# Opening of a streaming encoder on one core: place of the first value-weight transfer, and identity products on TensorE ahead of the first two tiles

## The reference, cut to what matters

```
hp = rms_norm(xp, norm_mix[0]);  hs = rms_norm(xs, norm_mix[0])
qkv = (xn @ w_qkv).reshape(b, t, 3, N_HEADS, HEAD_DIM)
s = einsum('bqhd,bkhd->bhqk', q, k) * scale + bias
p = softmax(s);  o = einsum('bhqk,bkhd->bqhd', p, v);  x = x + o @ w_o
```

## Time and profile before

| | |
|---|---|
| median of 3 runs | 1281.15 us (1277.71, 1281.42, 1281.15) |
| profiled execution, its own time | 1276.23 us |
| its span, first to last instruction | 1274.6 us |
| TensorE busy | 1072.0 us, 84% |
| VectorE, ScalarE, GpSimd busy | 493.7, 289.5, 272.3 us |
| chain that ended last | TensorE 58%, DMA 21%, VectorE 10%, issue 8% |
| mean granted TensorE clock | 0.931 of 2.4 GHz |

### The profile page before, as it was taken

The page is one execution under the profiler, slowest core; times in us unless marked ns, Lnnn a source line. Parts: engine busy times, 40 slices in busy tenths (PEclk is TensorE's granted clock), DMA queues, the critical chain, the costliest instruction groups (busy, mean ns, idle before and its releaser), DMA issues.

```text
span 1274.6 us, 14578 instructions
## 1 busy us (share of the span) xinstructions
PE 1072.0 (84%) x5326; PEld 621.2 (49%) x5326; DVE 493.7 (39%) x1066; ACT 289.5 (23%) x616; POOL 272.3 (21%) x289
## 2 busy tenths in 40 slices
PE   6999999998996978777746999987986978787780
PEld 5777777774545333333315777653544333333320
DVE  3234444344356211111115799984554111111116
ACT  3233232333111101000003455553111101000002
POOL 3000000001003211001051488850003111100033
PEclk9999999999997989888887999998996989998895
DMA  8953322302707999999955912000037999999963
GB/s 279 389 174 110 109 96 78 105 25 106 297 34 280 412 420 419 421 421 421 391 165 141 374 37 71 25 25 12 32 108 290 396 421 421 421 420 421 378 258 131
DMA packets 110287, 303.68 MB, mean 238 GB/s; under 512 B 18440, under 2 KB 65672, under 8 KB 86521
## 3 DMA queue, kind: packets, MB, share of 16 engines
q1 hardware_dynamic: 87977, 254.74, 51.8%
q0 software_dynamic: 22256, 48.22, 10.4%
HBM read 278.34 MB, written 57.12 MB: 263 GB/s over the span
## 4 chain that ended last, share of the span: by engine, by line
PE 58%; DMA 21%; DVE 10%; issue 8%; ACT 2%; SPq 1%; POOL 0%; DVEq 0%; POOLq 0%
PE bank L1205 12%; PE bank L522 10%; DMA ring<-in_w_up 8%; DMA arena<-in_w_up 8%; PE bank L421 7%; PE bank L1224 6%; PE bank L549 4%; DVE bank L1711 2%; PE bank L1507 2%; PE bank L572 2%; PE bank L1195 2%; PE bank L588 2%; PE bank L613 2%; PE bank L346 1%; DMA work<-in_w_pw 1%
## 5 line engine op out<-in xcount | busy, mean ns | idle before, releaser
L1205 PE MATMUL bank<-ring,work 128*64 128x512 f32 x704 | 170.1, 639 | 30.4 <-DMA ring<-in_w_up 28.6
L1224 PE MATMUL bank<-ring,work 128*64 128x512 f32 x528 | 125.5, 619 | 36.2 <-DVE work L1243 23.8
L1507 PE MATMUL bank<-arena,work 128*128 128x288 f32 x512 | 129.6, 416 | 8.0 <-issue 3.6
L522 PE MATMUL bank<-arena,ring 128*128 128x288 f32 x512 | 131.9, 412 | 0.4 <-issue 0.4
L1205 PEld LDWEIGHTS bank<-ring,work 128*64 128x64 f32 x704 | 58.4, 147 | 139.3 <-issue 136.9
L1239 DVE TENSOR_TENSOR work<-work,bank 128x256 f32<-128x256 f32 x33 | 13.9, 420 | 287.9 <-ACT work L1235 287.9
L1507 PEld LDWEIGHTS bank<-arena,work 128*128 128x128 f32 x512 | 99.2, 195 | 37.9 <-issue 8.0
L1658 POOL TENSOR_TENSOR ring<-ring 128x606 f32<-128x606 f32 x76 | 103.6, 1363 | 55.3 <-ACT ring L1607 45.7
L522 PEld LDWEIGHTS bank<-arena,ring 128*128 128x128 f32 x512 | 94.9, 190 | 33.0 <-issue 8.4
L421 PE MATMUL bank<-ring,arena 128*128 128x512 f32 x224 | 101.2, 605 | 6.6 <-ACT arena L1642 6.6
L1205 PE MATMUL bank<-arena,work 128*64 128x512 f32 x352 | 86.2, 646 | 19.7 <-DMA arena<-in_w_up 18.7
(11 more groups left out here) (258 smaller groups left out, 1297.7 us busy)
## 6 DMA issues: line engine op xcount, KB each, us to landing
ring<-in_w_down SPq DMA_DIRECT2D x32, 2048.0 KB, 24.5
ring<-in_w_gate SPq DMA_DIRECT2D x20, 2048.0 KB, 21.6
ring<-in_w_up SPq DMA_DIRECT2D x20, 2048.0 KB, 30.7
arena<-in_w_gate SPq DMA_DIRECT2D x10, 2048.0 KB, 22.5
arena<-in_w_up SPq DMA_DIRECT2D x8, 2048.0 KB, 32.8
ring<-in_w_qkv SPq DMA_DIRECT2D x24, 512.0 KB, 6.1
y_sorted<-gain POOLq DMA_DIRECT2D x8, 1536.0 KB, 5.7
work<-in_w_pw SPq DMA_DIRECT2D x16, 512.0 KB, 5.2
```

The costliest lines, as they stand in the source:

```text
L522: mm = nc.tensor.matmul(bank[b][:, 0:HT], wa[s][:, w, c, :], xt[:, c, h * HT:(h + 1) * HT], start=c == 0, stop=c == C - 1)
L1205: mm = nc.tensor.matmul(bank[2 + s][rr, :], xte[s][:, c, rr], wgu[g][:, :, e, c, :], start=c == 0, stop=c == C - 1)
L1224: mm = nc.tensor.matmul(bank[5 + h][rr, :], hts[:, c, rr], wdn[s][:, e, c, h * HALF:(h + 1) * HALF], start=c == 0, stop=c == FC - 1)
L1507: mm = nc.tensor.matmul(bank[banks[h][w]][:, 0:GT], wp[s][:, w, c, :], xt[:, c, h * GT:(h + 1) * GT], start=c == 0, stop=c == C - 1)
```

## The change: where the value weights are asked for, and 33 identity products

Three edits. The request for the value weights of pair 0 is made behind that for tile 1, so ahead of tiles 2, 3 and 4; the same 512 KB go to the same place. TensorE multiplies the identity by itself 30 times before the transposes of tile 0, and 3 times between the transposes of tile 0 and of tile 1, into bank 5, which is first used when the head pairs begin. `keep_running` takes the bank as an argument, and keeps its old one elsewhere.

```
             # attn_pe
+            keep_running(30, 5)
             for j in range(TILES):
+                if j == 1:
+                    keep_running(3, 5)
                 turn_pe(pe, 0, j)
...
             # attn_sync
-            sp.dma_start(wa[0][:, 2, :, :], wq[:, :, 2 * D:2 * D + P]).then_inc(wv_in, 16)
...
-        def keep_running(count):
+        def keep_running(count, b=3):
             for _ in range(count):
-                nc.tensor.matmul(bank[3][:, 0:P], ident[:], ident[:], start=True, stop=True)
+                nc.tensor.matmul(bank[b][:, 0:P], ident[:], ident[:], start=True, stop=True)
...
             # block.sync
                 if j == 0:
                     sp.dma_start(gain[:, 0, :], broadcast(norm_mix[0])).then_inc(gain_in, 16)
+                if j == 1:
+                    sp.dma_start(wa[0][:, 2, :, :], w_qkv[0, :, 2 * D:2 * D + P].rearrange("(p c) n -> p c n", c=C)).then_inc(wv_in, 16)
```

## The result

The changed kernel takes 1285.38 us (median of 11 runs, 1283.35 to 1289.09) against 1281.42 us for the kernel before, measured beside it (11 runs, 1277.71 to 1284.12). The ratio is 1.0029, 95% interval 1.0017 to 1.004: 3.7 us slower, with 2.2 to 5.1 us in the interval (the two medians are 4.0 us apart; the ratio is an estimate over all runs). Forecast were 2.25 us. Its profiled execution took 1285.83 us, with a span of 1284.2 us.

What follows compares the result with a forecast made beforehand. It took q0's wait for pair 0's cached keys, landing at 29.09 us behind bias_rows, to cancel the opening's gain; 0 for all three edits plus 2.25 us for the clock on 1280.6 gave 1282.9 us, range 1277.5 to 1286.5.

Steps and rivals of the forecast that it cites:

- what bounds the opening: Before q0: the 0.43 us hole marked issue is the wait for pair 0's cached keys, landing at 29.09 us.
- The second rival: At q0: it doesn't wait for the keys, 3.4 us gained, time 1277.2 us; chance 0.08.
- Fillers, tile 0, tile 2, end of the opening: TensorE's opening: fillers end 11.5, tile 0 turned 11.5, tile 2 normed 16.05, last value product ends 25.6 us.
- The clock's cost: q0 to k1, 64 records: clock falls behind 3.5 us of idle, costing 2.25 us (bounds 0 and 3.0).
- The value weights cost nothing: Request order on the DMA queue: bias_rows and cached keys land unchanged, 0 us at 29.09, plus or minus 0.5.
- a sign of being wrong: At q0: prediction is wrong if q0 starts before 28 us or the keys' landing moves by more than 1 us.
- The last rival: Opening's transfers: keys land later as DMA engines run dry; from 1.6 us on, 1284.5 us and more; chance 0.08.
- The sum: Whole kernel: 0 for weights, fillers and earlier value products, plus 2.25 us for the clock; 1282.9 us, 0.18% slower.
- the third rival: Fillers before tile 0: they stay at 1.2 GHz and take 14.1 us; time 1282.1 to 1296 us; chance 0.04.
- a cap of 3.5 us: Pair 1's projection: its keys land at 42.8 us, projection starts at 46.38, limiting the second rival's gain.

Runs made afterwards that it cites:

- the bridge: Changed kernel with 18 more identity products between the last value product and q0: ratio 1.0014 to the kernel before.
- weights alone: Kernel before with only the value weights' request moved behind tile 1, no identity products: ratio 1.0034 to the kernel before.
- fillers alone: Kernel before with only the 33 identity products, value weights requested in their old place: ratio 1.003 to the kernel before.
- changed, keys early: Changed kernel with the request for pair 0's cached keys ahead of bias_rows: ratio 1.0003 to the kernel before.
- changed, keys and pair 1 early: Changed kernel with pair 0's cached keys ahead of bias_rows and pair 1's loads ahead of the wait for bias_rows: ratio 0.9968 to the kernel before.
- before, keys and pair 1 early: Kernel before with pair 0's cached keys ahead of bias_rows and pair 1's loads ahead of the wait for bias_rows: ratio 0.9997.
- fillers alone, small bridge: Kernel before with the 33 identity products and 6 more between the last value product and q0: ratio 1.0006 to the kernel before.

## Why the prediction was right, point by point

**The hole is the wait for the keys: right.** Step "what bounds the opening". The prediction had 0.43 us of issue in one row, and a start that fits a landing to 0.13 us; in the changed kernel the fit is 0.07 us (30.68, 30.75), and the move of the keys alone removed the hole. The second rival (q0 doesn't wait) is out.

**Fillers, tile 0, tile 2, end of the opening: right within 0.2 us.** Forecast 11.5, 11.5, 16.05, 25.6; measured 11.6, 11.48, 16.09, 25.72. The end of the fillers was partly luck. The granted clock column is 1.00 throughout, but the number of records in equal windows (in the brackets) tells when the clock rises:

```profile
5.00:7.00 2.00, 2.00 (x12) 1.00 0.78 295
7.00:7.50 0.50, 0.50 (x4) 1.00 1.01 352
7.50:8.00 0.50, 0.50 (x6) 1.00 0.96 372
8.00:10.00 2.00, 2.00 (x20) 1.00 0.98 310
```

It rises near 7.4 us, 5.3 us after the start, later than the 4.05 and 5 taken from the earlier trace rows; and by the starts of its records an identity product takes 0.43 us before and 0.22 behind, less than the 0.47 and 0.24 taken from the value products. The two errors nearly cancel.

**The clock's cost: right in kind, nearly in size.** 2.25 forecast from one row of the same form, 2.01 measured in the profile and 1.9 by the bridge. The worked kernel of the Trainium skill ("TensorE: Matmul & The Clock Gate", the section on how oscillation bites in real kernels) would have given an estimated 0.8; the three losses of a run of these products behind a hole that profiles show here are 1.7, 1.7 and 2.0 us (17.45 and 17.77 against 15.76, 5.84 against 4.15), and the measurement decides.

**The value weights cost nothing: this step failed, by about a microsecond.** The term "0 us at 29.09, plus or minus 0.5" held that the landing is bound by the bytes ahead of it and that their order does not matter. The bytes are the same, but the new order moves fewer of them from 13 to 17 us, and `bias_rows` lands 1.1 us later between the means of the profiles. The keys landed at 30.68, 1.6 us later than in the one profile of before that was at hand, and 1.2 later than the mean of its three profiles (29.09, 29.3, 30.0). Either is more than the 1 us that the prediction itself named as a sign of being wrong, and q0 did not start at 29.2. The last rival had this direction and a threshold of 1.6 us, but another mechanism, a queue run dry; the DMA share from 13 to 17 us is 1.15 or 1.16 with the new order and 1.19 or 1.20 with the old, so it did not run dry, it moved fewer bytes while busy.

**The sum: the right result by two terms where one was forecast.** 2.0 for the clock and 1.1 for q0's later start are 3.1 us, which is the whole shift of the first score product against the mean of three profiles. The measured 3.7 (2.2 to 5.1) holds it. The forecast 1282.9 us was placed on a base of 1280.6; against the 1281.42 measured beside the change it would have been 1283.7. The measured 1285.38 lies 0.4 above the forecast's own range (1280.6 to 1285), inside the whole one (to 1286.5), and nearer to the last rival's "1284.5 and more" than to the forecast. The direction held, clear of noise. The verdict of no change by 0.3% held by 0.01%, with nearly half of the interval beyond it: that is luck. In the third rival 16.2 and 14.1 make 30.3 and not 30.7, so its lower price would be 1281.7; nothing else hangs on it.

**Does the opening account for the runs?** The end of the last value product of attention (L613) against the mean of the three profiles of before (318.05), beside what the runs measured, in us:

| kernel | end of attention | runs (95% interval) |
|---|---|---|
| changed kernel | +3.1 | +3.7 (2.2 to 5.1) |
| weights alone | +3.0 | +4.4 (2.6 to 6.1) |
| fillers alone | +0.6 | +3.8 (2.3 to 5.5) |
| changed, 18 more fillers | +1.3 | +1.8 (0 to 3.6) |
| changed, keys early | +0.2 | +0.4 (-1.4 to 2.2) |
| changed, keys and pair 1 early | -3.9 | -4.1 (-6.1 to -2.2) |
| the same with 20 fillers | -4.4 | -5.4 (-7.3 to -3.5) |
| the same without fillers | -2.4 | -1.9 (-3.6 to -0.3) |
| the same, old place of the weights | -3.0 | +0.1 (-1.5 to 1.7) |
| before, keys and pair 1 early | -0.3 | -0.4 (-1.9 to 1.0) |
| fillers alone, small bridge | +0.4 | +0.8 (-0.8 to 2.3) |

In nine of eleven the shift lies inside the interval of the runs. The two that don't have fillers ahead of a wait for the value weights and no bridge, and their cause stays open, as said above.

**Not foreseen: the second wait.** The prediction computed a cap of 3.5 us for pair 1 from its keys' landing at 42.8, and used it for a rival only. With the opening moved it decided: those keys landed at 47.8 in the changed kernel.

## What to carry to other kernels

A hole of a few tenths of a microsecond between two instructions, marked "issue", deserves the landing times of everything its semaphore counts. Where a wait sums several transfers, a small one behind the largest in the queue can be the one that decides, as the 64 KB of keys behind 3 MB did here. Speeding up the engine in front of such a wait only makes the hole longer, and a longer hole can cost the clock (2.0 us here). Move the small request first; then ask at once what waits next, since there were two in a row here, and the gain was to be had only with both gone.

## What the runs showed of the hardware that was not expected

- With 512 KB in rows of 512 bytes asked for ahead of three tiles in rows of 4 KB, the queue moved as much by 12 us as with the old order (304 to 306 GB/s in three profiles, 305 to 308 in five), but only 192 to 211 GB/s from 13 to 17 us instead of 282 to 290, at nearly the same busy share (1.15 or 1.16, and 1.19 or 1.20). A lower rate in one window can be a change of places; compare the bytes moved by a later time as well.
- The granted clock column read 1.00 through the whole opening of the kernel before, while the durations showed 1.2 GHz until about 20 us; in the changed kernel it read 1.00 over the rise near 7.4 us as well. In these openings only the duration of a known product told the clock.
- The first rise of the clock under fillers came at very different points: the same 30 products took from 8.39 to 9.90 us in seven profiles.
- The clock fell behind a wait of only 2.05 us at pair 1 (16 records in 5.84 us instead of 4.15) and behind one of 2.03 us at value product 0, and held over one of 1.34 us at the same place.
